# Building the compression MLP's input by strided views of TensorE's moving operand, against a copied window

## The reference, cut to what matters

```
def compress(kv, pe, w1, w2):            # kv: [B, 512, 2 groups, 64]
    blocks = ...                         # 31 windows of 32 tokens, one every 16 tokens
    blocks = blocks + pe[None, None, :, None, :]
    flat = blocks.transpose(0, 3, 1, 2, 4).reshape(B, G, nc, CMP_LEN * dh)   # [2, 31, 2048]
    return jax.nn.silu(flat @ w1) @ w2   # w1: 2048 x 256, w2: 256 x 64
```

## Time and profile before

| | us |
|---|---|
| median of three executions | 2803.85 |
| lowest and highest | 2801.32, 2804.14 |
| the profiled execution, its own time | 2804.14 |
| its span in the trace | 2801.9 |

### The profile page before, as it was taken

The page is one execution under the profiler, slowest core; times in us unless marked ns, Lnnn a source line. Parts: engine busy times, 40 slices in busy tenths (PEclk is TensorE's granted clock), DMA queues, the critical chain, the costliest instruction groups (busy, mean ns, idle before and its releaser), DMA issues.

```text
span 2801.9 us, 20731 instructions
## 1 busy us (share of the span) xinstructions
PE 2183.1 (78%) x6440; PEld 1028.0 (37%) x6440; DVE 1735.5 (62%) x3670; ACT 764.2 (27%) x2125; POOL 622.5 (22%) x540
## 2 busy tenths in 40 slices
PE   5999999999999999999899555556555656546564
PEld 3454545444444444454567311122211222112121
DVE  5434475211124115123449998999989989999987
ACT  2022344010000002222323333333333333233332
POOL 0000000000000000000014444444444444444443
PEclk9999999999999999999999767768777786777767
DMA  9521011211246311211039999999999999999997
GB/s 373 218 95 61 31 61 35 86 60 60 90 177 254 138 71 65 97 42 57 16 150 370 388 421 419 416 388 422 417 414 405 406 409 420 415 385 414 422 420 328
DMA packets 85498, 694.58 MB, mean 248 GB/s; under 512 B 9489, under 2 KB 9489, under 8 KB 10513
## 3 DMA queue, kind: packets, MB, share of 16 engines
q0 software_dynamic: 77184, 587.24, 51.4%
q1 hardware_dynamic: 7200, 98.57, 9.3%
q10 hardware_dynamic: 1008, 7.52, 0.7%
HBM read 691.19 MB, written 2.10 MB: 247 GB/s over the span
## 4 chain that ended last, share of the span: by engine, by line
PE 48%; DMA 23%; DVE 20%; issue 6%; POOL 2%; ACT 1%; POOLq 0%; DVEq 0%; ACTq 0%
PE PS L449 21%; DMA arena<-in_peer_uv,arena 19%; PE PS L479 8%; DVE arena L1708 6%; PE PS L908 4%; DVE arena L1696 3%; PE PS L954 3%; DMA ring<-in_peer_uv,arena 3%; DVE ring L1696 3%; POOL arena L1780 2%; PE PS L634 2%; PE PS L654 1%; PE PS L643 1%; PE PS L515 1%; PE PS L929 1%
## 5 line engine op out<-in xcount | busy, mean ns | idle before, releaser
L1243 PE MATMUL PS<-ring,arena 128*128 128x512 f32 x472 | 370.5, 931 | 363.0 <-ACT arena L1395 331.8
L1780 POOL DMA_INDIRECT arena<-in_peer_uv,arena x276 | 334.3, 1211 | 834.2 <-DVE arena L1678 487.4
L1243 PE MATMUL PS<-arena 128*128 128x512 f32 x480 | 317.9, 802 | 169.7 <-ACT arena L1395 169.6
L449 PE MATMUL PS<-arena,ring 128*128 128x512 f32 x832 | 371.8, 606 | 9.1 <-DVE arena L1487 4.9
L1696 DVE CUSTOM_DVE_ANT_0 arena<-arena 128x1024 f32<-128x1024 f32 x276 | 334.6, 1227 | 56.6 <-DMA arena<-in_peer_uv,arena 55.8
L1780 POOL DMA_INDIRECT ring<-in_peer_uv,arena x236 | 275.1, 1166 | 371.0 <-DVE arena L1708 284.5
L1243 PEld LDWEIGHTS PS<-ring,arena 128*128 128x128 f32 x472 | 120.0, 280 | 595.5 <-ACT arena L1395 492.8
L1388 ACT ACTIVATE arena<-arena 128x1 f32<-128x1 f32 x512 | 103.0, 201 | 832.3 <-DVE arena L1696 831.7
L1696 DVE CUSTOM_DVE_ANT_0 ring<-ring,arena 128x1024 f32<-128x1024 f32 x236 | 283.1, 1222 | 54.6 <-DMA ring<-in_peer_uv,arena 50.1
L449 PE MATMUL PS<-hT,ring 128*128 128x256 f32 (+1 forms) x944 | 310.2, 489 | 7.2 <-ACT hT L339 3.6
L1243 PEld LDWEIGHTS PS<-arena 128*128 128x128 f32 x480 | 113.2, 252 | 373.9 <-ACT arena L1395 260.1
(11 more groups left out here) (276 smaller groups left out, 2421.5 us busy)
## 6 DMA issues: line engine op xcount, KB each, us to landing
ring<-in_wstream SPq DMA_DIRECT2D x46, 2048.0 KB, 7.4
arena<-in_ada POOLq DMA_DIRECT2D x24, 2048.0 KB, 8.4
arena<-in_peer_uv,arena POOLq DMA_INDIRECT x276, 9.7
ring<-in_peer_uv,arena POOLq DMA_INDIRECT x236, 9.4
xT<-in_xT ACTq DMA_DIRECT2D x1, 2048.0 KB, 14.2
arena<-in_alibi ACTq DMA_DIRECT2D x1, 2048.0 KB, 11.9
result<-arena SPq DMA_DIRECT2D x4, 512.0 KB, 8.2
arena<-in_subkeys ACTq DMA_DIRECT2D x1, 1024.0 KB, 4.9
```

Of the source, the lines that this page charges most:

```text
L449: ins = pe.matmul(o, l, r, start=(a == 0), stop=(a == len(lhs) - 1))
L1243: ins = pe.matmul(bank(6 + b), diag[:, k % NDIAG, :], rows[slot_of(n)][:, D + b * 512:D + (b + 1) * 512], start=opens, stop=closes)
L1780: pool.indirect_dma_start(rows[j], None, ap["peer_uv"], bass.IndirectOffsetOnAxis(ap=eidx[:, t, e:e + 1], axis=0)).then_inc(landed[j], 16)
```

## The change

The packed windows `win` are gone. DVE's copies into `stk` stay; `stk[r]` gets a third plane, which is set to zero and then receives the 16 columns of the position parameter, two elements apart. PE's operands change places: a 128x128 tile of the weight block is now the stationary operand, and the moving operand is a view of `stk[r]` of 3 planes by 31 elements, 16 elements apart, 93 columns in all. The hidden layer so comes out with its 256 units on partitions, in two halves of 128 (hc = 0, 1), and needs no transpose. Column 62 of it is the product of the position parameter with the weights; the columns after it are not used. DVE copies that column of both halves to `hb`, and ACT adds it as the bias of the SiLU, in two instructions of 128x62. The second, small product of r = 0 now stands in PE's program ahead of the matmuls of r = 1, where before both r's large products came first. `hid` is used for both.

```
-        stk = [area(108, 2, S), area(112, 2, S)]
-        win = [area(100, 16, 2, NC), area(104, 16, 2, NC)]
+        stk = [area(108, 3, S), area(114, 3, S)]
...
             for r in range(2):
                 n = BLOCK0["ck"] + r
                 block_arrived(pe, n)
                 w = ring[n % 2][:, :].rearrange("p (l m) -> p l m", l=16)
-                pe.wait_ge(c_win, 2 * r + 2)
-                for l in range(16):
-                    ins = pe.matmul(PS[64 * r:64 * r + 62, 2 + r, 0:256], win[r][:, l, :, :].rearrange("p g j -> p (g j)"), w[:, l, :],
-                                    start=(l == 0), stop=(l == 15))
+                if r == 0:
+                    pe.wait_ge(c_stk, 10)
+                for hc in range(2):
+                    for l in range(16):
+
+                        rhs = stk[r][:, :, 2 * l:2 * l + 16 * (NC - 1) + 1:16]
+                        ins = pe.matmul(PS[:, 2 * r + hc, 0:3 * NC].rearrange("p (g j) -> p g j", g=3), w[:, l, tile(hc)],
+                                        rhs, start=(l == 0), stop=(l == 15))
                 ins.then_inc(mm_done, 1)
-            for r in range(2):
-                q = slice(64 * r, 64 * r + 62)
-                pe.wait_ge(c_hid, r + 1)
-                for hc in range(2):
-                    ins = pe.transpose(PS[:, 4 + r, 62 * hc:62 * hc + 62], hsil[q, tile(hc)], ident[q, q])
-                ins.then_inc(c_turn, 1)
...
+                pe.wait_ge(c_hid, 2 * r + 2)
+                if r == 0:
+                    (the four small calls with ck2, as before)
+                else:
+                    (the four small calls with cv2, as before)
...
-                act.wait_ge(mm_done, MM0["ck"] + r + 1)
-                act.activation(hsil[q, :], PS[q, 2 + r, 0:256], ACT.Silu).then_inc(c_hid, 1)
+                act.wait_ge(c_pe, 1 + r)
+                act.wait_ge(c_mm, r) if r else None
+                for hc in range(2):
+                    act.activation(hid[:, hc * 62:(hc + 1) * 62], PS[:, 2 * r + hc, 0:2 * NC], ACT.Silu,
+                                   bias=hb[:, hc:hc + 1]).then_inc(c_hid, 1)
...
-                dve.wait_ge(c_stk, 4 * r + 4)
-                for a in range(2):
-                    (two additions from stk into win, L1464)
+                own(dve.memset(stk[r][:, 2, :], 0.0))
+                dve.tensor_copy(stk[r][:, 2, 0:32:2], prow("pek" if r == 0 else "pev")).then_inc(c_stk, 1)
...
             for r in range(2):
-                dve.wait_ge(c_turn, r + 1)
-                dve.tensor_copy(hid if r == 0 else hidv, PS[:, 4 + r, 0:124]).then_inc(c_copy, 1)
+                dve.wait_ge(mm_done, MM0["ck"] + r + 1)
+                if r:
+                    dve.wait_ge(c_hid, 2)
+                dve.tensor_copy(hb, PS[:, 2 * r:2 * r + 2, 2 * NC]).then_inc(c_pe, 1)
+                dve.wait_ge(c_mm, r + 1)
+                (and the copies out to kcT and vcm, as before)
```

More of the change, by code:

```diff
@@ L197, in build @@
         rt = area(118, 2, S)
-        stk = [area(108, 2, S), area(112, 2, S)]
-        win = [area(100, 16, 2, NC), area(104, 16, 2, NC)]
-        hsil = area(96, 256)
-        hidv = area(97, 124)
+        stk = [area(108, 3, S), area(114, 3, S)]
         adaw = [area(32, BLK), area(48, BLK)]
@@ L255, in build @@
         hid = small(0, 124)
+        hb = small(124, 2)
         kcT = small(126, NC)
@@ L1001, in build @@
         g_sig, g_turn = sem("gates_sigmoid"), sem("gates_turned")
-        c_stk, c_win, c_hid, c_turn, c_copy, c_mm = (
-            sem(n) for n in ("cmp_stacked", "cmp_windows", "cmp_silu", "cmp_turned", "cmp_copied", "cmp_out"))
+        c_stk, c_mm, c_pe, c_hid, c_out = (sem(n) for n in ("cmp_stacked", "cmp_hidden", "cmp_bias", "cmp_silu", "cmp_out"))
         y_tmp = sem("y_tmp")
@@ L1094, in _ @@
[L1094 to L1105, removed]
@@ L1106, in _ @@
-            ins.then_inc(c_mm, 1)
+                if r == 0:
[5 more added lines that the diff above has]
+                                        rhs, start=(l == 0), stop=(l == 15))
+                ins.then_inc(mm_done, 1)
@@ new lines, in _ @@
+                pe.wait_ge(c_hid, 2 * r + 2)
+                if r == 0:
+                    for g in range(NG):
+                        for hc in range(2):
+                            ins = pe.matmul(PS[g * DH:(g + 1) * DH, 0, 128:128 + NC], prow("ck2", hc * DH, (hc + 1) * DH),
+                                            hid[:, hc * 62 + g * NC:hc * 62 + (g + 1) * NC], start=(hc == 0), stop=(hc == 1))
+                    ins.then_inc(c_mm, 1)
+                else:
+                    for g in range(NG):
+                        for hc in range(2):
+                            ins = pe.matmul(PS[0:NC, 1, 128 + g * DH:128 + (g + 1) * DH],
+                                            hid[:, hc * 62 + g * NC:hc * 62 + (g + 1) * NC],
+                                            prow("cv2", hc * DH, (hc + 1) * DH), start=(hc == 0), stop=(hc == 1))
+                    ins.then_inc(c_mm, 1)
@@ L1470, in _ @@
             for r in range(2):
-                dve.wait_ge(c_turn, r + 1)
-                dve.tensor_copy(hid if r == 0 else hidv, PS[:, 4 + r, 0:124]).then_inc(c_copy, 1)
[L1473 to L1476, removed]
+                dve.wait_ge(mm_done, MM0["ck"] + r + 1)
[3 more added lines that the diff above has]
+                dve.wait_ge(c_mm, r + 1)
+                if r == 0:
+                    own(dve.tensor_copy(kcT, PS[:, 0, 128:128 + NC]))
+                else:
+                    own(dve.tensor_copy(vcm[0:NC, :], PS[0:NC, 1, 128:256]))
             fence(dve, "dve")
```

## The result

The changed kernel takes 2819.62 us (median of six executions, 2816.98 to 2826.97) against 2802.85 for the kernel before (six executions, 2800.64 to 2808.25). The ratio is 1.0060, with a 95% interval of 1.0046 to 1.0076: slower by 0.6%, some 17 us, where the prediction had 3 us more and a range that ended at 2815. The profiled executions are 2816.59 and 2804.14 us, 12.45 us apart.

What follows compares the result with a forecast made beforehand. PE was taken as the bound, 48% of the chain that ended last. The terms -0.8 - 0.2 + 2.6 - 0.3 + 1.8 = +3.1 us on 2804.14, less 0.3 to the median, gave 2806.9 us; range 2802 to 2815.

Steps and rivals of the forecast that it cites:

- DVE ahead of the fence: Before the large product: fewer DVE additions let PE use its idle time at the spread, -0.8 us (-0.7 to -1.1).
- The large product: PE's hidden-layer matmuls: 128 records at 0.109 us, paced by weight loads, 14.0 us in all, -0.2 us.
- rival A: Large product: strided moving operand read slowly, 1.65 ns a column, +8.7 in all, 2812.5 us; chance 0.30, beyond that 0.06.
- The stall: Between r = 0 and r = 1: PE waits for bias copy, table load, SiLU and small calls, +2.6 us (2.4 to 3.0).
- The tail: From the end of r = 1's large product to the first attention score: 2.0 us instead of 2.3, -0.3 us.
- The clock: Under the stream of r = 1: one more fall of PE's clock after the stall, +1.8 us (0 to 3.6).
- The sum: Over the whole kernel: all terms together +3.1 us, passed on to the end, giving 2806.9 us.
- Rivals B and C: B: no clock fall, 2805.1 us, chance 0.14; C: large product's weight loads wholly under the streams, 2801.5 us, chance 0.10.

Runs made afterwards that it cites:

- e1: The changed kernel with each plane's 31 moving elements read packed instead of 16 apart (wrong windows, same work): ratio 1.0035 to the kernel before.
- e4: The changed kernel without the third plane in the moving operand, 62 columns a call instead of 93, same step: 2813.25 us, one execution.
- e5: The changed kernel with the moving operand read packed and both large products ahead of the small ones: ratio 1.0002 to the kernel before.
- e8: The kernel before with packed windows as moving operand, 128x128 weights stationary, no transposes, r = 1 windows made later by DVE: 2800.88 us, ratio 0.9990.
- e3: The changed kernel with both large products ahead of the small ones, strided reading kept: ratio 1.0027 to the kernel before.
- e7: The changed kernel with three unused 512-column matmul calls between r = 0's large product and the wait for its SiLU: ratio 1.0038 to the kernel before.
- e9: The kernel before with the transposes and small product of r = 0 put between its two large products, operands unchanged: ratio 1.0012.
- e6: The changed kernel with both large products first and steps of 3, 5, 8 and 16 elements in the moving operand: 2807.36 us, one execution.
- e11: The changed kernel with a one-column SiLU ahead of ACT's first wait, so the table load runs early: ratio 1.0047 to the kernel before.

## Why the prediction was wrong, by its own steps

- **DVE ahead of the fence, -0.8.** Right: 0.96, inside the bounds, and PE no longer idles ahead of the spread.
- **The large product, -0.2.** This is the first of two steps that failed. Its condition, "if the reading of the moving operand keeps up", was not met, and its bounds of 12.8 to 14.2 us held only under it. The floor that weight loads set was well read (0.109 forecast; 0.112 to 0.113 measured in e1, e4, e5 and e8), but the strided columns take more. At full clock the two products cost 20.7 us (e3), +6.5. That is rival A, and the row it rested on was near: 1.65 ns a column from DVE's L1464, 1.7 measured on PE. That the two agree so well is in part luck: they are two engines with other paces, and no run says why they should be alike. Rival A got 0.36 of the chance and should have been the forecast: it was the only row that read with this step, and what I held against it was not a row.
- **The stall, +2.6.** Right in place and size: 2.86, of which 0.22 because the small product ran at half clock already.
- **The tail, -0.3.** At half clock the gain did not come: 2.33. At full clock (e3: 192.59 - 190.66 = 1.93) it is -0.4.
- **The clock, +1.8 (0 to 3.6).** The fall was foreseen, in its place and with its cause: e7 shows that filling the stall takes it away. What failed, the second step, is its price. It was read from a stream of 512 columns, in which the clock was soon back, and carried over to one in which it was not. It cost 3.5 us in r = 1 (13.96 and 10.48 in e7), 0.22 in L1093, about 0.4 in the tail and 1.44 in L632 and L906, 5.6 in all. e9 gives what the forecast had in mind, 1.67 us for a fall before 256-column records. Even before 512 columns 1.8 is no fixed price: in e6 the fall at the first score made L634 1.51 and L908 6.61 us, 3.3 in all against e3's 1.08 and 3.70. And the split between this term and the large product is a choice: at half clock packed records would have been as slow (0.213 us, e1), so of the 6.8 us that r = 1 lost, 3.4 can be put down to either.
- **The sum.** With the sizes that the runs showed, -0.96 + 6.5 + 2.6 - 0.4 + 5.6 is 13.3; measured are 12.13 up to the first score and 1.44 after it, 13.57. Neither failed step alone would have left the range: with the large product at +6.5 the forecast is 2813.6, with the clock at +5.6 it is 2810.7, with both 2817.4. So rival A, at 2812.5, was right in its mechanism and still short of 2819.62.
- **Rivals B and C** fell: the clock fell in every kernel with an unfilled stall, and the records of the large product came no faster than 0.11 us each.

What stays open: the profiled executions are 12.45 us apart and the medians 16.8. The profiled execution of the changed kernel is the fastest of its seven, that of the kernel before the slowest but one of six, which may be some of it. The repeated trace of the changed kernel has the same stretch to 0.01 us, and e11 took 2812.8 to 2813.9 in three executions and 2818.9 to 2819.7 in three. The 14 traces show where single executions differ: from the second scores to the first gather it is 1253.0 to 1259.6 us, and from there to the end 1349.3 to 1355.0, in kernels that have the same program there. What causes it was not traced. Nor was it tried whether 128x128 loads with more columns, or smaller loads with few, bring the clock back; only the two kinds of stream named above were compared.

## What to carry to other kernels

Before turning a packed operand into a view, price the view: on PE a 93-column fp32 record with a 128x128 weight load went from 0.113 to between 0.160 and 0.172 us once its elements lay 16 bytes apart or more, while 62 columns 64 bytes apart cost nothing, as the weight loads were longer. A stall between the large products cost its length and, in every one of the seven traces where it was left unfilled, a fall of the clock. That fall's price has to be read from the stream that comes after it: 1.7 us before 256-column records (e9), 5.6 before thin ones. So keep independent large products together ahead of dependent small ones, or fill the gap.

## What was not expected of the hardware

A step of 2 fp32 elements was as good as packed (0.114 us a record), 3 nearly (0.127), and 4, 5, 8 and 16 cost about the same (0.160 to 0.172), the widest least. At granted clock 0.50 a record with a 128x128 load took 0.213 us, read from the starts, with 93 strided columns, with 93 packed ones and with 62 strided ones alike. So the strided reading did not take twice as long at half clock, which would be 0.320: its price does not follow the clock as the stream's other costs do. The clock stayed at half for 24 us while PE was busy nearly all the time (13.61 of 14 us from 184 to 198).
